# Strassen's seven block products over half of the depth in three wide gate-and-value projections

## The reference

```python
def swiglu(u, w_in, w_out):
    a, v = jnp.split(u @ w_in, 2, axis=-1)
    return (jax.nn.silu(a) * v) @ w_out

def ffn_sublayer(h, shift, scale, gate, w_in, w_out, g, b):
    y = swiglu(modulate(h, shift, scale), w_in, w_out)
    return layer_norm(ALPHA * h + FFN_RES * gate * y, g, b)
```

## Time and profile before

| | |
|---|---|
| median of three runs | 2618.56 us |
| profiled execution | span 2618.0 us; the page gives no other time of it, 0.6 us under the median |
| TensorE busy | 2574.1 us, 98% of the span |
| VectorE, ScalarE, GpSimd busy | 1688.2, 1093.9, 445.0 us |
| granted TensorE clock | 0.9 or more in each of the 40 slices |
| chain that ended last | TensorE 89%, VectorE 5%, ScalarE 3% |

### The profile page before, as it was taken

One profiled execution on the slowest core, in us unless ns is written; L12 is line 12 of the kernel. 1 busy time (PEld: TensorE's weight loads), 2 busy tenths in 40 slices (PEclk: granted clock), 3 DMA queues, 4 the chain that ended last, 5 costly groups with the idle time before them and its releaser, 6 DMA issues.

```text
span 2618.0 us, 43371 instructions
## 1 busy us (share of the span) xinstructions
PE 2574.1 (98%) x17000; PEld 2287.9 (87%) x17000; DVE 1688.2 (64%) x2582; ACT 1093.9 (42%) x1560; POOL 445.0 (17%) x491
## 2 busy tenths in 40 slices
PE   8999999999999999999999999999999999999999
PEld 6888888867888888888889889989999999998999
DVE  6766747466674474675574876666866666675565
ACT  4222224265422222321223674345655555565453
POOL 4000024122500003400004232020201201100210
PEclk9999999999999999999999999999999999999999
DMA  7554523411253252354452225445433554542554
GB/s 297 169 184 154 190 106 132 159 65 49 97 197 132 97 202 79 129 197 149 146 191 76 88 76 190 177 153 222 164 128 125 182 192 173 194 160 81 180 188 156
DMA packets 64762, 394.40 MB, mean 151 GB/s; under 512 B 7552, under 2 KB 9056, under 8 KB 29664
## 3 DMA queue, kind: packets, MB, share of 16 engines
q1 hardware_dynamic: 43872, 317.17, 33.9%
q0 software_dynamic: 20192, 73.21, 8.5%
q10 hardware_dynamic: 544, 1.88, 0.2%
...
## 4 chain that ended last, share of the span: by engine, by line
PE 89%; DVE 5%; ACT 3%; issue 1%; DMA 1%; POOL 1%; SPq 0%; DVEq 0%; ACTq 0%; POOLq 0%
PE banks L459 24%; PE banks L461 23%; PE banks L460 23%; DVE wlo L384 2%; ACT whi L376 2%; PE banks L479 1%; PE banks L481 1%; PE banks L480 1%; PE banks L1787 1%; PE banks L1774 1%; DMA scale_start<-in_w_mod_scale 1%; PE banks L598 1%; PE banks L599 1%; PE banks L600 1%; PE banks L1763 1%
## 5 line engine op out<-in xcount | busy, mean ns | idle before, releaser
L384 DVE TENSOR_TENSOR wlo<-raw,whi 128x2048 fp32r<-128x2048 f32 (+1 forms) x262 | 641.0, 2447 | 341.1 <-ACT whi L376 341.0
L376 ACT CAST whi<-raw 128x2048 fp32r<-128x2048 f32 (+1 forms) x264 | 533.8, 2022 | 387.4 <-PE banks L461 355.3
L459 PE MATMUL banks<-uhi,whi 128*128 128x512 f32 (+2 forms) x1520 | 552.4, 363 | 2.9 <-DVE sums L2091 1.5
L460 PE MATMUL banks<-ulo,whi 128*128 128x512 f32 (+2 forms) x1520 | 551.3, 363 | 0.0
L461 PE MATMUL banks<-uhi,wlo 128*128 128x512 f32 (+2 forms) x1520 | 551.3, 363 | 0.0
L459 PE MATMUL banks<-u2hi,whi 128*128 128x256 f32 x1248 | 351.5, 282 | 2.1 <-DVE wlo L384 2.0
L460 PE MATMUL banks<-u2lo,whi 128*128 128x256 f32 x1248 | 348.5, 279 | 0.0
L461 PE MATMUL banks<-u2hi,wlo 128*128 128x256 f32 x1248 | 348.3, 279 | 0.0
L643 DVE SCALAR_TENSOR_TENSOR squares<-mod_slot,crow 128x1024 f32<-128x1024 f32 x256 | 313.3, 1224 | 31.0 <-DMA mod_slot<-in_w_mod 7.7
L459 PEld LDWEIGHTS banks<-uhi,whi 128*128 128x128 f32 x1520 | 285.6, 188 | 54.1 <-issue 1.8
L461 PEld LDWEIGHTS banks<-uhi,wlo 128*128 128x128 f32 x1520 | 285.6, 188 | 50.1
...
## 6 DMA issues: line engine op xcount, KB each, us to landing
raw<-in_ffn_in SPq DMA_DIRECT2D x132, 1024.0 KB, 4.8
...
mod_slot<-in_w_mod POOLq DMA_DIRECT2D x128, 512.0 KB, 3.7
raw<-in_w_merge SPq DMA_DIRECT2D x32, 1024.0 KB, 4.8
raw<-in_w_in SPq DMA_DIRECT2D x26, 1024.0 KB, 4.7
raw<-in_na_qkv SPq DMA_DIRECT2D x12, 1024.0 KB, 4.7
raw<-in_w_out SPq DMA_DIRECT2D x8, 1024.0 KB, 4.7
raw<-in_wa_qkv SPq DMA_DIRECT2D x6, 1024.0 KB, 4.8
```

Of the source, the lines that this page charges most:

```text
L376: act.copy(whi[u % 2][:, 0:unit_size[u]], raw[u % 2][:, 0:unit_size[u]]).then_inc(hi_done, 1)
L384: dve.tensor_tensor(wlo[u % 2][:, 0:n], raw[u % 2][:, 0:n], whi[u % 2][:, 0:n].bitcast(F32), ALU.subtract).then_inc(lo_done, 1)
L459: pe.matmul(out, w_hi, x_hi[:, k, 0:T], start=(n == 0), stop=False)
L460: pe.matmul(out, w_hi, x_lo[:, k, 0:T], start=False, stop=False)
```

## The change

Only in1 of the three wide feed-forwards changes its arithmetic (33 units). Over feature chunks 0 to 3 the product of weights (4 chunks x 2 halves) and activations (4 chunks x 2 token groups) is a 2x2 by 2x2 product of blocks, and is formed with seven block products instead of eight. Each block product is 2 feature chunks x 3 matmuls by 256 tokens. Chunks 4 to 7 stay as they are.

- GpSimd adds and subtracts blocks of the raw weights, 4 operations of 256 elements a unit, in place and in the free columns 2048 to 2815 of `raw`. The cast waits for it. Cast and subtraction of these units are 2816 wide instead of 2048.
- Sums of blocks of the activations are formed once a feed-forward: 9 GpSimd operations of 512 elements beside in0 and behind it, 4 ScalarE casts and 4 VectorE subtractions of 512 elements in out0, behind the second unit.
- The results are put together from four banks: ScalarE copies one product, VectorE has four operations of 256 elements and two of 512, all reading a bank, before silu and product.
- Modulation chunks are dealt out anew, and no loop is left in in1.

Cut to its core (PE, ACT and DVE stages, and the places of the modulation):

```diff
+FAST = ("L0.ffn0.in1", "L0.ffn1.in1", "L1.ffn0.in1")
...
-        act.wait_ge(landed[u % 2], plus(16 * (u // 2 + 1), 16, it))
+        if u in fast_units:
+            act.wait_ge(*POOL_.at("weight sums", u))
+        else:
+            act.wait_ge(landed[u % 2], plus(16 * (u // 2 + 1), 16, it))
...
+    FAST_MODS = {"L0.ffn0": ((3, 3, 3, 3), (2, 1, 1, 1, 1, 1, 1, 1, 1, 1, 1), (4,)),
+                 "L0.ffn1": ((2, 2, 2, 2), (0, 1, 0, 1, 0, 1, 0, 1, 0, 0, 0), (4,)),
+                 "L1.ffn0": ((2, 3, 3, 3), (1, 1, 0, 1, 1, 1, 0, 1, 1, 1, 1), (4,))}
...
+    def input_sums_act(act, name):
+
+        act.wait_ge(*POOL_.at("input sum", name, 3))
+        for k in range(4):
+            act.copy(SUMS_HI[k], SUMS[k]).then_inc(*ACT_.up(("input sum hi", name, k)))
...
+    def input_sums_dve(dve, name):
+
+        for k in range(4):
+            dve.wait_ge(*ACT_.at("input sum hi", name, k))
+            dve.tensor_tensor(SUMS_LO[k], SUMS[k], SUMS_HI[k].bitcast(F32), ALU.subtract)\
+                .then_inc(*DVE_.up(("input sum lo", name, k)))
...
+    def weight_sums_pool(pool, u):
...
+        pool.wait_ge(landed[u % 2], 16 * (u // 2 + 1))
...
+        pool.tensor_tensor(s3, first[:, :, 0], first[:, :, 1], ALU.add).then_inc(*POOL_.up())
+        pool.wait_ge(*POOL_.here())
+        pool.tensor_tensor(first[:, :, 1], first[:, :, 1], second[:, :, 1], ALU.add).then_inc(*POOL_.up())
+        pool.wait_ge(*POOL_.here())
+        pool.tensor_tensor(v, first[:, :, 1], first[:, :, 0], ALU.add).then_inc(*POOL_.up())
+        pool.wait_ge(*POOL_.here())
+        pool.tensor_tensor(w, second[:, :, 0], v, ALU.add).then_inc(*POOL_.up(("weight sums", u)))
...
+        for u in range(ph.u0, ph.u0 + ph.n):
...
+            start_unit(pe, u)
+            fast_product(pe, u, carry[:, 0:S], A11, quarter(uhi, 0, 0), quarter(ulo, 0, 0))
+            fast_product(pe, u, carry[:, S:T2], V, SUMS_HI[1], SUMS_LO[1]).then_inc(*PE_.up(("carry", u)))
+            fast_product(pe, u, last[:, S:T2], U, SUMS_HI[0], SUMS_LO[0])
+            fast_product(pe, u, last[:, 0:S], S3, SUMS_HI[2], SUMS_LO[2])
+            plain_rest(pe, u, 0)
+            fast_product(pe, u, gate_[:, 0:S], A12, quarter(uhi, 1, 0), quarter(ulo, 1, 0), False, False)
+            fast_product(pe, u, gate_[:, S:T2], W, quarter(uhi, 1, 1), quarter(ulo, 1, 1), False)\
+                .then_inc(product, 1)
+            plain_rest(pe, u, 1)
+            fast_product(pe, u, value[:, 0:S], A22, SUMS_HI[3], SUMS_LO[3], False).then_inc(product, 1)
...
+    def fast_in_act(act, name):
...
+            if i < ph.n:
+                split_hi(act, u + 1)
+            if i:
+                act.wait_ge(*DVE_.at("hidden", u - 1))
+                act.copy(fhi[:, i - 1, :], hidden[:, (u - 1) % 2, :]).then_inc(f_hi, 1)
+            if i < ph.n:
+                act.wait_ge(*PE_.at("carry", u))
+                act.wait_ge(f_split, f - 1)
+                act.copy(silu_a[:, u % 2, 0:S], banks[:, carry_bank(u), 0:S]).then_inc(*ACT_.up(("first product", u)))
+                act.wait_ge(*DVE_.at("gate", u))
+                act.activation(silu_a[:, u % 2, :], silu_a[:, u % 2, :], ACT.Silu).then_inc(f_silu, 1)
+
+    def fast_in_dve(dve, name):
...
+            if i:
+                v = u - 1
+                full = hidden[:, v % 2]
+                dve.wait_ge(product, 2 * v + 2)
+                dve.wait_ge(*DVE_.at("value", v))
+                dve.tensor_tensor(full, banks[:, bank(v, 1), :], full, ALU.subtract).then_inc(evicted, 1)
+                dve.wait_ge(evicted, v + 1)
+                dve.wait_ge(f_silu, f)
+                dve.tensor_tensor(full, silu_a[:, v % 2], full, ALU.mult).then_inc(*DVE_.up(("hidden", v)))
+            if i < ph.n:
+                for n in fast_mods(name[:7], 1, i):
+                    mod_products(dve, n)
+                if i or name != "L0.ffn0.in1":
+                    split_lo(dve, u + 1)
+            if i:
+                dve.wait_ge(f_hi, f)
+                dve.tensor_tensor(flo[:, i - 1, :], full, fhi[:, i - 1, :].bitcast(F32), ALU.subtract)\
+                    .then_inc(f_split, 1)
...
+                dve.wait_ge(product, 2 * u + 1)
...
+    def fast_in_pool(pool, name):
+        ph, tag = phases[name], name[:7]
+        loads = fast_mods(tag, 0)
+        for n in loads[:-2]:
+            mod_load(pool, n)
+        for i in range(2):
+            weight_sums_pool(pool, ph.u0 + i)
+            mod_load(pool, loads[i - 2])
+        for i in range(2):
+            mod_load(pool, fast_mods(tag, 1)[i])
+        for i in range(ph.n):
+            if i + 2 < ph.n:
+                weight_sums_pool(pool, ph.u0 + i + 2)
+            for n in fast_mods(tag, 1, i):
+                mod_load(pool, n + 2)
+        for n in fast_mods(tag, 2)[2:]:
+            mod_load(pool, n)
...
+            if name[:7] in FAST_MODS and name.endswith(".out1") and i == 0:
+                for n in fast_mods(name[:7], 2):
+                    mod_products(dve, n)
...
-            if name in MOD_FIRST:
-                for n in range(MODS_PER_UNIT[name]):
-                    if name == "L0.ffn0.out0" and i == ph.n - 1 and n == 1:
+            if name[:7] in FAST_MODS:
+                if name.endswith(".out0") and i == 1:
+                    input_sums_dve(dve, name[:7] + ".in1")
+                for k, n in enumerate(fast_mods(name[:7], 0, i) if name.endswith(".out0") else ()):
+                    if name == "L0.ffn0.out0" and i == ph.n - 1 and k == 1:
                         split_lo(dve, u + 2)
-                    mod_products(dve, MOD_FIRST[name] + MODS_PER_UNIT[name] * i + n)
+                    mod_products(dve, n)
```

More of the change, by code:

```diff
@@ new lines, in build, with carry_bank, fast_product @@
+    A11, U, A12, A22, S3, V, W = (lambda j: j * 256, lambda j: j * 256 + P, lambda j: (2 + j) * 256,
+                                  lambda j: (2 + j) * 256 + P, lambda j: 2048 + j * P, lambda j: 2304 + j * P,
+                                  lambda j: 2560 + j * P)
+    def carry_bank(u):
+        return 4 + 2 * (u % 2)
+    def fast_product(pe, u, out, weights, x_hi, x_lo, start=True, stop=True):
+        for j in range(2):
+            w_hi, w_lo = (t[u % 2][:, weights(j):weights(j) + P] for t in (whi, wlo))
+            pe.matmul(out, w_hi, x_hi[:, j], start=(start and j == 0), stop=False)
+            pe.matmul(out, w_hi, x_lo[:, j], start=False, stop=False)
+            mm = pe.matmul(out, w_lo, x_hi[:, j], start=False, stop=(stop and j == 1))
+        return mm
@@ new lines, in plain_rest, with fast_in_pe @@
+    def plain_rest(pe, u, half):
+        out = banks[:, bank(u, half), :]
+        for k in range(4, KC):
+            w_hi, w_lo = cols(whi, u, k, half * P, half * P + P), cols(wlo, u, k, half * P, half * P + P)
+            pe.matmul(out, w_hi, uhi[:, k], start=(k == 4), stop=False)
+            pe.matmul(out, w_hi, ulo[:, k], start=False, stop=False)
+            pe.matmul(out, w_lo, uhi[:, k], start=False, stop=False)
+    def fast_in_pe(pe, name):
+        ph = phases[name]
+        pe.wait_ge(*DVE_.at("input sum lo", name, 3))
+        for u in range(ph.u0, ph.u0 + ph.n):
+            gate_, value, carry, last = (banks[:, b] for b in (bank(u, 0), bank(u, 1), carry_bank(u), carry_bank(u) + 1))
+            start_unit(pe, u)
[9 more added lines that the diff above has]
+            fast_product(pe, u, value[:, 0:S], A22, SUMS_HI[3], SUMS_LO[3], False).then_inc(product, 1)
@@ L1726, in block1_ffn @@
         if engine == "pool":
-            for part in ("in0", "out0", "in1"):
-                if f"{tag}.{part}" in MOD_FIRST:
-                    mod_loads(e, f"{tag}.{part}")
+            if f"{tag}.in0" in MOD_FIRST:
+                mod_loads(e, f"{tag}.in0")
             if T == T2:
+                input_sums_pool(e, f"{tag}.in1")
+                fast_in_pool(e, f"{tag}.in1")
                 if s == 3:
```

89 lines of the change are left out of this document (86 added, 3 removed).

## The result

The changed kernel takes **2657.59 us** (median of four runs, 2655.86 to 2658.02), the kernel before 2618.40 beside it. The ratio is 1.0145, 95% interval 1.0131 to 1.0160: 39 us slower. The forecast was 2620.5 with a range to 2634, so the result lies outside the range, and slower where no change was forecast. The profiled execution after has a span of 2655.7 us, 37.7 above that of before.

What follows compares the result with a forecast made beforehand. TensorE, busy 98% of the span, was taken as the bound. -23.1 + 2 x 2.8 + 2 x 2.7 + 7.0 + 5.9 + 1.2 = +2.0 us gave 2620.5 us, no change that can be told, range 2603 to 2634.

Steps and rivals of the forecast that it cites:

- The products, -23.1: In1's 33 units: each shortens from 11.20 to 10.50 us, 0.70 us a unit, -23.1 us in all.
- 9 GpSimd operations ... lie beside in0, where GpSimd only issues loads: Input sums beside in0: nine GpSimd operations of 512 elements, twice 0.77 us each, with no wait priced.
- O2 to O3, 2 x 2.8: Out0 of L0.ffn0 and L1.ffn0: lo part of O4 starts later behind the input sums, +2.8 us each.
- O4 to I1, 2 x 2.7: Entry to in1 in L0.ffn0 and L1.ffn0: TensorE waits for the weights' sums, +2.7 us each.
- S+18.1: S is O4's start; I1's lo part ends 18.1 us later, where TensorE is ready at S+15.4.
- The backlogs, 7.0 and 5.9: I1 to I3: VectorE's queued work delays I3 by 7.0 us in L0.ffn0 and I2 by 5.9 in L1.ffn0.
- meetings: GpSimd and VectorE operations meeting in the two backlogs: 0.2 us each, three a phase, +1.2 us in all.
- The steady state, 9.7 against 10.5: In1 units: VectorE needs 9.7 us with a chunk against TensorE's 10.5, so TensorE stays the bound.
- The rival that VectorE becomes the bound: In1: weights' sums on GpSimd slow VectorE to 11.6 us a unit; 2634.5 us, up to 2650; chance 0.20.
- The vectors "lie under the cast for P4": Behind P2 in out1: a dozen VectorE operations on 8 to 24 columns, hidden under the cast for P4.
- Nowhere in L0.ffn1: Sign for the changed trace: TensorE waits for the lo part in L0.ffn0 and L1.ffn0, never in L0.ffn1.
- the rule that the two engines shut each other out: In1: each weights' sum holds VectorE its whole 0.77 us, 3.1 us a unit; 2650 us; 0.05 of the rival's 0.20.

Runs made afterwards that it cites:

- s3: s1 plus vectors before P1's read-outs, and out0/in1 modulation products of L0.ffn0 and L1.ffn0 cut to 8 of 1024 elements: 2599.99 us, ratio 0.9929.
- s1: Changed kernel with seven of nine input sums spread over in0 and the first two out0 loads issued before the last two sums: 2634.64 us, ratio 1.0057.
- e6: Changed kernel with twenty extra matmuls of 512 columns into an unused bank in place of the waits in front of O1: 2649.27 us.
- e2: Changed kernel with GpSimd's four sums of each unit's weights replaced by one copy of 16 elements: 2649.08 us.
- e3: Changed kernel without GpSimd's input sums and with its weights' sums replaced by one small copy: 2629.13 us.

## Why the prediction was wrong

- **The products, -23.1:** right, 22.4 measured. 10.52 us a unit, and s3 reaches 2600.0. The rows' spacing held; by the cycles that the Trainium skill gives for an isolated matmul (TensorE: Matmul & The Clock Gate, Back-to-back issue gap) a unit would have gained 0.60 us, and 0.68 were measured.
- **"9 GpSimd operations ... lie beside in0, where GpSimd only issues loads":** this step failed first. It looked at what GpSimd does there and not at VectorE, which in in0 has the most to do. Three waits of 5.0 us, 15.1 us, were priced at nothing; s1 took all of them away by place alone. (Alone a sum has 1.29 us, not twice 0.77.)
- **What a wait costs:** the sum took each wait at its length. Beside eight of them the clock stands at half for 3 to 10 us, and the starts of the matmuls lost 14.8 us there, of the 18.2 that the waits' lengths don't cover. e6 shows it at three of them, 5.8 us; the 3.3 behind O4 stand in place of waiting in front of I1. With the O1 waits it is the term that was missing.
- **O2 to O3, 2 x 2.8:** right in place and size, 2.36 and 2.52.
- **O4 to I1, 2 x 2.7:** right in place and mechanism; its terms add up to S+17.9, not S+18.1. Measured were 1.07 and 1.18, yet not because the sums were free: two of the four have 1.6 to 1.7 us there, where 0.75 is their time alone. The clock's fall behind O4 kept TensorE busy for 1.6 us of the wait. Where it did not fall the wait is 2.60 to 2.67 us, and where the sums are out (e2, e3) there is none.
- **The backlogs, 7.0 and 5.9:** the mechanism was right (e2, without meetings: 6.34 and 5.55), the meetings were mis-sized. They cost 2.2 and 2.9, not 0.6 each.
- **The steady state, 9.7 against 10.5:** with the sums it is 11.27. The rival that VectorE becomes the bound was true in mechanism (11.6 expected) but small in itself: 3 x 0.47. It mattered through the backlogs and in front of I1, and all of it, with the clock behind, is the 8.5 us of e2.
- **The vectors "lie under the cast for P4":** wrong by 2.6 us and the clock behind it; the norm's sums on GpSimd begin at that place.
- **"Nowhere in L0.ffn1":** true from O1 on; its gain of 7.5 was there. The wait in front of it was not foreseen.

Against the measured +38.2 at the end of P4, from +2.0: O1 waits +15.1, clock and what is not a listed wait +18.2, backlogs +2.8, P4 +2.6, units +1.4, entries -3.2, O4 -0.7. The result lies beyond the 2634 to 2650 of the rival with VectorE as the bound, and came by another way: that rival had no wait in front of O1 and no cost of the clock.

The prediction gave 0.05 to the rule that the two engines shut each other out (the Trainium skill, SBUF, State Buffer: Who interferes with whom). The rows above bear it out in kind: VectorE's two-input operations are held, its reads of banks are not, and the one-input copies and scalar operations behind P2, of 8 elements, are held to the end of a GpSimd operation that has begun. The size is what differed from my working: a 256-element sum holds for 0.42 to 0.53 us of its 0.75, so 1.5 us a unit, not 3.1. And I weighed the rule only for in1, not for the input sums or the vectors, where the same sentence would have shown the loss.
